# Halved loads and a re-ordered scatter in the expert loop of a two-block transformer kernel

## The reference

```
idx, gate = top 8 of 64 experts a token (4 of 8 groups), gates scaled to sum 2.5
y_rows    = (silu(xb @ w_gate[e]) * (xb @ w_up[e])) @ w_down[e] * gate      # 1024 -> 256 -> 1024
routed    = zeros(256, 1024).at[row_tok].add(y_rows)                        # the scatter
x         = x + g2 * (routed + shared(h))
out       = rmsnorm(x, final_g)
```

## Time and profile before

| | |
|---|---|
| median of 3 runs | 1319.68 us (1318.68 to 1320.43) |
| profiled execution | 1322.26 us, span 1320.6 us, mean granted clock 0.997 |
| TensorE busy | 1291.8 us (98%) |
| VectorE, ScalarE, GpSimd busy | 708.1, 254.1, 147.7 us |
| moved by DMA | 356.45 MB, mean 270 GB/s |

### The profile page before, as it was taken

How to read it: one execution, slowest core, us unless ns; L and a number is a source line. 1 busy time by engine, 2 the same in 40 slices (tenths; PEclk the granted TensorE clock), 3 DMA queues, 4 the chain that set the end, 5 groups by cost and what they waited for, 6 DMA issues and landing times.

```text
span 1320.6 us, 20050 instructions
## 1 busy us (share of the span) xinstructions
PE 1291.8 (98%) x7744; PEld 801.0 (61%) x7744; DVE 708.1 (54%) x1308; ACT 254.1 (19%) x586; POOL 147.7 (11%) x133
## 2 busy tenths in 40 slices
PE   9999999999999999999999999999999999999997
PEld 8667675875879566686685765744344444444432
DVE  1235589778789669968878574622222222222223
ACT  2144311201211251111122152310000000000002
POOL 1125500000011432000000902000000000000000
PEclk9999999999999999999999999999999999999999
DMA  9940154664533346675683414599999999999995
GB/s 381 362 155 34 65 194 168 244 226 176 204 126 130 142 177 243 248 301 194 262 310 147 154 70 169 222 420 420 420 421 421 421 420 420 421 421 421 420 422 224
DMA packets 51219, 356.45 MB, mean 270 GB/s; under 512 B 5936, under 2 KB 6208, under 8 KB 9536
## 3 DMA queue, kind: packets, MB, share of 16 engines
q1 hardware_dynamic: 45456, 321.45, 60.5%
q0 software_dynamic: 5392, 32.05, 6.6%
q10 hardware_dynamic: 288, 1.80, 0.3%
HBM read 353.73 MB, written 1.05 MB: 269 GB/s over the span
## 4 chain that ended last, share of the span: by engine, by line
PE 87%; DVE 7%; DMA 2%; issue 2%; ACT 1%; DVEq 0%; SPq 0%; ACTq 0%
PE ps L1089 13%; PE ps L1625 13%; PE ps L1080 11%; PE ps L1603 6%; PE ps L1654 6%; PE ps L1562 5%; PE ps L856 4%; PE ps L1370 4%; PE ps L1037 4%; PE ps L939 2%; PE ps L1019 2%; PE ps L1363 2%; PE ps L960 2%; DMA y_rows<-in_stream 2%; PE ps L895 1%
## 5 line engine op out<-in xcount | busy, mean ns | idle before, releaser
L3099 DVE TENSOR_TENSOR masked_and_probs<-ps,gate_rows 128x512 f32<-128x512 f32 x52 | 33.6, 686 | 143.9 <-PE ps L1654 142.5
L1603 PE MATMUL ps<-masked_and_probs,probT 128*128 128x512 f32 x208 | 94.4, 594 | 0.1
L3089 DVE TENSOR_TENSOR masked_and_probs<-masked_and_probs,ps 128x256 f32<-128x256 f32 x26 | 11.0, 421 | 153.9 <-ACT masked_and_probs L2163 153.9
L1080 PEld LDWEIGHTS ps<-xT,ring 128*128 128x128 f32 x768 | 87.7, 192 | 4.9 <-issue 4.9
L1080 PE MATMUL ps<-xT,ring 128*128 128x128 f32 x768 | 88.8, 275 | 0.8 <-issue 0.8
L1089 PE MATMUL ps<-ring,qk_tiles 128*128 128x512 f32 x192 | 85.2, 592 | 0.0
L1796 ACT ACTIVATE qk_tiles<-ps 128x512 f32<-128x512 f32 (+7 forms) x58 | 30.2, 522 | 256.4 <-PE ps L1080 248.5
L2163 ACT ACTIVATE masked_and_probs<-ps 128x256 f32<-128x256 f32 x26 | 10.0, 383 | 348.5 <-PE ps L1625 348.5
L1625 PE MATMUL ps<-ring,vec_rows 128*32 128x512 f32 (+2 forms) x312 | 64.9, 592 | 0.0
L1562 PE MATMUL ps<-masked_and_probs,mix_rows 128*128 128x256 bf16 (+1 forms) x384 | 61.9, 269 | 0.7 <-ACT v_rows L2139 0.7
L1089 PEld LDWEIGHTS ps<-ring,qk_tiles 128*128 128x128 f32 x192 | 35.8, 190 | 41.6 <-issue 41.6
(11 more groups left out here) (549 smaller groups left out, 2595.0 us busy)
## 6 DMA issues: line engine op xcount, KB each, us to landing
ring<-in_stream SPq DMA_DIRECT2D x201, 1024.0 KB, 9.9
qk_tiles<-in_stream SPq DMA_DIRECT2D x38, 1024.0 KB, 21.0
v_rows<-in_ada POOLq DMA_DIRECT2D x12, 1024.0 KB, 5.6
qk_tiles<-in_ada POOLq DMA_DIRECT2D x12, 1024.0 KB, 6.2
vec_rows<-in_stream SPq DMA_DIRECT2D x12, 1024.0 KB, 19.9
par<-in_stream SPq DMA_DIRECT2D x12, 1024.0 KB, 16.9
y_rows<-in_stream SPq DMA_DIRECT2D x12, 1024.0 KB, 17.3
xT<-in_stream SPq DMA_DIRECT2D x12, 1024.0 KB, 20.3
```

The source lines that it names most:

```text
L1080: mm = pe.matmul(ps[:, bank, m * P:(m + 1) * P], weights[:, kk, m * P:(m + 1) * P], tokens[:, kk, :], start=fresh and m == 0 and kk == 0, ...
L1603: mm = pe.matmul(ps[:, q, :], probT[:, buf, 256 + q // 2 * P:256 + (q // 2 + 1) * P], yslot[:, q % 2 * 512:(q % 2 + 1) * 512], start=False ...
L3099: dve.tensor_tensor(yslot[:, cols], ps[:, 5 + half, :], gaterow[:, 1, cols], ALU.mult).then_inc(ready, 1)
```

## The change

Four edits, all in or behind the loop:

- Loads. The up chunk comes in two row halves (all four first halves, then all four second halves; the second ones count in `s_rear`), with a wait in front of the products of its last two row groups. The halves of the down chunk are no longer row halves but column halves: each takes 512 columns of both k, so two runs of 2 KB a partition. 20 loads an iteration instead of 16, same bytes.
- Down by column halves. `down_units(half)` makes one half of the columns with both k; the second call waits for `s_second`.
- Scatter. Quarters 0 and 2 of the last static block go ahead of the loop, behind a wait for `s_ya`; 1 and 3 between gate and up. Quarters 0 and 2 of the loop's own rows go between the two down halves, behind waits for `s_tsb` and `s_ya`; 1 and 3 come behind the next iteration's gate products, or behind the loop. The gather, the transposes and the waits for the copies have no scatter beside them any more.
- Final squares and gains run in the order 0, 2, 1, 3; one semaphore replaces two.

```diff
+        s_rear = sem("rear_rows_loaded")
...
-                for n in range(2 * PER_MORE):
-                    c, a = divmod(n, PER_MORE)
-                    sp.wait_ge(s_late, it * LOOPED + (n + 1))
-                    load(LOOP_SLOTS[n][0], ids[a] * 3 + (RINGED + c))
+                for a in range(PER_MORE):
+                    sp.wait_ge(s_late, it * LOOPED + (a + 1))
+                    load(LOOP_SLOTS[a][0], ids[a] * 3 + RINGED)
                 for half in range(2):
                     cols = slice(half * D, (half + 1) * D)
+                    for a in range(PER_MORE):
+                        slot = LOOP_SLOTS[PER_MORE + a][0]
+                        if half == 0:
+                            sp.wait_ge(s_late, it * LOOPED + (PER_MORE + a + 1))
+                        sp.dma_start(moe_slot(slot)[:, cols],
+                                     d_stream[bass.ds(ids[a] * 3 + (RINGED + 1), 1)].rearrange("o p c -> (o p) c")[:, cols]
+                                     ).then_inc(s_rear if half else m_full[slot], 16)
+                for half in range(2):
+                    cols = slice(half * 512, (half + 1) * 512)
                     for a in range(PER_MORE):
                         n = 2 * PER_MORE + a
                         slot = LOOP_SLOTS[n][0]
                         if half == 0:
                             sp.wait_ge(s_late, it * LOOPED + (n + 1))
-                        sp.dma_start(moe_slot(slot)[:, cols],
-                                     d_stream[bass.ds(ids[a] * 3 + (RINGED + 2), 1)].rearrange("o p c -> (o p) c")[:, cols]
+                        sp.dma_start(moe_slot(slot).rearrange("p (k n) -> p k n", k=2)[:, :, cols],
+                                     d_stream[bass.ds(ids[a] * 3 + (RINGED + 2), 1)].rearrange(
+                                         "o p (k n) -> (o p) k n", k=2)[:, :, cols]
                                      ).then_inc(s_second if half else m_full[slot], 16)
...
-            def scatter(buf, quarters=range(4), last=False):
+            def scatter(buf, quarters=range(4)):
                 for q in quarters:
-                    if last and q == 1:
-                        pe.wait_ge(s_yv, more + NB)
                     mm = pe.matmul(ps[:, q, :], probT[:, buf, 256 + q // 2 * P:256 + (q // 2 + 1) * P],
                                    yslot[:, q % 2 * 512:(q % 2 + 1) * 512], start=False, stop=False, skip_group_check=True)
-                    if last:
-                        mm.then_inc(s_moe, 1)
+                return mm
...
-            def down_units(slots, buf, it):
-
+            def gate_up_units(slots, it):
+
+                pe.wait_ge(s_hga, it + (2 * PAIRS + 1))
+                pe.wait_ge(s_hgv, it + (2 * PAIRS + 1))
+                for c in range(2):
+                    ws = []
+                    for a in range(PER_MORE):
+                        slot, full = slots[c * PER_MORE + a]
+                        pe.wait_ge(m_full[slot], full)
+                        ws.append(moe_slot(slot).rearrange("p (k n) -> p k n", k=4))
+                    for kk in range(4):
+                        if c == 1 and kk == 2:
+                            pe.wait_ge(s_rear, it * (16 * PER_MORE) + 16 * PER_MORE)
+                        for a, ((lo, width),) in enumerate(UNIT_TILES):
+                            mm = pe.matmul(ps[lo:lo + width, 4, :], hg[:, 4 * c + kk, lo:lo + width], ws[a][:, kk, :],
+                                           start=c == 0 and kk == 0, stop=c == 1 and kk == 3, skip_group_check=True)
+                            if kk == 3:
+                                mm.then_inc(s_late, 1)
+                    if c == 0:
+                        pe.wait_ge(s_yv, it + NB)
+                        scatter(act_buf, (1, 3))
+
+            def down_units(half, slots, buf, it):
+
+                if half:
+                    pe.wait_ge(s_second, it * (16 * PER_MORE) + 16 * PER_MORE)
                 ws = []
-                for a, tiles in enumerate(UNIT_TILES):
+                for a in range(PER_MORE):
                     slot, full = slots[2 * PER_MORE + a]
                     pe.wait_ge(m_full[slot], full)
                     ws.append(moe_slot(slot).rearrange("p (k n) -> p k n", k=2))
                 for k in range(2):
-                    if k == 1:
-                        pe.wait_ge(s_second, it * (16 * PER_MORE) + 16 * PER_MORE)
-                    for half in range(2):
-                        for a, ((lo, width),) in enumerate(UNIT_TILES):
-                            mm = pe.matmul(ps[lo:lo + width, 5 + half, :], probT[:, buf, k * P + lo:k * P + lo + width],
-                                           ws[a][:, k, half * 512:(half + 1) * 512], start=k == 0, stop=k == 1,
-                                           skip_group_check=True)
-                            if k == 1:
-                                mm.then_inc((s_downhalf, s_late)[half], 1)
+                    for a, ((lo, width),) in enumerate(UNIT_TILES):
+                        mm = pe.matmul(ps[lo:lo + width, 5 + half, :], probT[:, buf, k * P + lo:k * P + lo + width],
+                                       ws[a][:, k, half * 512:(half + 1) * 512], start=k == 0, stop=k == 1,
+                                       skip_group_check=True)
+                        if k == 1:
+                            mm.then_inc((s_downhalf, s_late)[half], 1)
...
             act_buf = (NB - 1) % 2
+            pe.wait_ge(s_tsb, NB)
+            pe.wait_ge(s_ya, NB)
+            scatter(act_buf, (0, 2))
             with pe.Fori(0, more) as it:
                 slots = [(slot, it * 16 + 16 * (loads + 1)) for slot, loads in LOOP_SLOTS]
                 pe.wait_ge(s_tsb, it * 2 + NB)
                 pe.wait_ge(s_sel, it + (PAIRS + 1))
                 gather_units()
-                pe.wait_ge(s_ya, it + NB)
-                pe.wait_ge(s_yv, it + NB)
-                scatter(act_buf, range(1))
-                pe.wait_ge(s_hga, it + (2 * PAIRS + 1))
-                pe.wait_ge(s_hgv, it + (2 * PAIRS + 1))
-                gate_up(UNIT_TILES, slots, [s_late] * LOOPED, [hg[:, 0:4, :], hg[:, 4:8, :]])
-                scatter(act_buf, range(1, 3))
+                gate_up_units(slots, it)
                 pe.wait_ge(s_hid2, it + (NB + 1))
                 turn_hidden_rows().then_inc(s_tps, 1)
-                scatter(act_buf, range(3, 4))
-
                 turn_weights(unit_selectw, 4).then_inc(s_tps, 1)
                 pe.wait_ge(s_tsb, it * 2 + (NB + 1))
-                down_units(slots, act_buf, it)
-            pe.wait_ge(s_ya, more + NB)
-            pe.wait_ge(s_tsb, more * 2 + NB)
-            scatter(act_buf, last=True)
+                down_units(0, slots, act_buf, it)
+                pe.wait_ge(s_tsb, it * 2 + (NB + 2))
+                pe.wait_ge(s_ya, it + (NB + 1))
+                scatter(act_buf, (0, 2)).then_inc(s_moe, 1)
+                down_units(1, slots, act_buf, it)
+            pe.wait_ge(s_yv, more + NB)
+            for q in (1, 3):
+                scatter(act_buf, (q,)).then_inc(s_moe, 1)
...
-                act.wait_ge(s_moe, q + 1)
...
-            for q in range(4):
-                square_quarter(q)
+            act.wait_ge(s_moe, more)
+            square_quarter(0)
+            square_quarter(2)
+            act.wait_ge(s_moe, more + 1)
+            square_quarter(1)
+            act.wait_ge(s_moe, more + 2)
+            square_quarter(3)
             std()
-            act.wait_ge(s_root, 1)
-            act.wait_ge(s_gained, 3)
+            act.wait_ge(s_gained, 4)
             for t in range(TT):
                 first_half_out(t)
...
-            def gain_quarter(q):
+            def gain_quarter(q, squares):
                 t, cols = q // 2, slice((q % 2) * 512, (q % 2 + 1) * 512)
-                dve.wait_ge(s_ss, 5 + q + 1)
+                dve.wait_ge(s_ss, 5 + squares)
                 dve.tensor_tensor(y[:, t, cols], ps[:, q, :], vec[:, 1, cols], ALU.mult).then_inc(s_gained, 1)
             link(dve.memset(guard, RMS_EPS))
             dve.wait_ge(s_vecA, 64)
             dve.wait_ge(s_vecB, 80)
-            for q in range(3):
-                gain_quarter(q)
+            gain_quarter(0, 1)
+            gain_quarter(2, 2)
+            gain_quarter(1, 3)
             link(dve.tensor_tensor(guarded, quarter_ms[:, :, 0], guard.to_broadcast([P, TT]), ALU.add))
             dve.wait_ge(s_ss, 5 + 4)
             norms[0] += 1
             dve.tensor_tensor(var2, quarter_ms[:, :, 1], guarded, ALU.add).then_inc(s_var, 1)
             dve.wait_ge(s_std, norms[0])
             inv_sqrt(rstd, var2, std2, nwt)
-            dve.engine_nop().then_inc(s_root, 1)
+            dve.engine_nop().then_inc(s_gained, 1)
             dve.wait_ge(s_gained, 3)
```

More of the change, by code:

```diff
@@ L424, in build @@
         s_gated = sem("shared_down_gated")
-        s_root = sem("last_inverse_roots")
-        s_gained = sem("last_rows_by_gain")
```

(1 more changed line is left out.)

## The result

The changed kernel took 1326.64 us in the median of 5 runs (1324.84 to 1329.47), the kernel before, beside it, 1320.13 (1318.68 to 1320.43): ratio 1.0054, 95% interval 1.0039 to 1.0069, so 6.5 us between the medians. Run twice more it gave 1.0052 (1.0039 to 1.0066) and 1.0053 (1.0040 to 1.0067). The forecast was 1325.5, range 1323.2 to 1328.2.

What follows compares the result with a forecast made beforehand. The prediction took the order of TensorE's own work, not the loads, to bound the kernel. Its terms 2.71 + 0 + 1.72 - 0.64 + 1.99 gave +5.8 us on the median 1319.68: 1325.5 us, range 1323.2 to 1328.2.

Steps and rivals of the forecast that it cites:

- Bound: End of the kernel: the order of TensorE's own work sets the end; weight loads are early by 3.4 and 1.8 us.
- Step 1: Ahead of the loop: a 0.99 us wait for VectorE's half plus four scatter slots delay the gather, +2.71 us.
- step 3: Gate to up: four scatter slots now stand between the products, their waits long met, +1.72 us.
- step 4: End of up to start of down: no scatter fills it, the dependent chain takes 2.58 instead of 3.22 us, -0.64.
- step 5: Down halves and scatter alternate: TensorE needs each half right after making it, 4.59 us a leg, +1.99 us.
- second sum, by waits: TensorE's idle time grows by 0.99, 0.86 behind the gather, about 2.1 around transposes, 2 x 1.15 less 0.29 at the end.
- Step 7: Loads: 2 KB segments at some 385 GB/s, last landing 1306.5, needed at 1314.1, 0 us; upper bound 1.8.
- Rival D: Loads: 2 KB segments run at half rate or worse, +1.8 us on top, 1327.3 us; chance 0.03.
- step 2: Gather to gate: stays 4.89 us though emptied of scatter, 0 us; bounds -0.49 and +0.2.
- rival A: New tail: short gaps halve TensorE's clock, losing 1.5 us (1327.0) to 6.9 us (1332.4); chance 0.10.
- Rival B: Loop's second-half loads: the last landing sets the end, so the change gains 0.86 us, 1318.8 us; chance 0.04.
- Rival C: Three waits for VectorE's halves (0.99, 1.15, 1.15) cost nothing, leaving +2.5 us, 1322.2 us; chance 0.06.

Runs made afterwards that it cites:

- experiment 2: Kernel before with the change's loads and merged semaphore, TensorE's old order kept: 1320.50 us against 1320.50, ratio 1.0001.
- 3: Changed kernel with the loads of the kernel before, so only the new order of work: 1325.54 us against 1320.50, ratio 1.0036.
- 4: Changed kernel with quarters 0 and 2 of the last static block moved between gather and gate: 1323.56 us against 1320.33, ratio 1.0024.
- 6: Changed kernel with quarters 1 and 3 behind the up products instead of between gate and up: 1324.06 us against 1320.33, ratio 1.0029.
- 5: Changed kernel with the two down halves back to back, quarters 0 and 2 behind them: 1324.41 us against 1320.33, ratio 1.0031.
- 10: Changed kernel with all scatter quarters set into existing waits and down halves back to back: 1319.74 us against 1320.50 before, ratio 0.9997.
- experiment 9: Changed kernel plus six small ScalarE copies lengthening the gap between gather and gate: 1325.49 us against 1320.22 before, ratio 1.0047.
- experiment 7: Changed kernel plus two unread 128x512 products between gather and gate, run twice: 1326.31 and 1326.27 us, ratios 1.0042 and 1.0048 to before.
- experiment 11: Changed kernel with scatter quarters in existing waits, down halves together, final squares released one by one: 1318.36 us against 1320.22 before, ratio 0.9989.

## Why the prediction was right

Measured step by step in the trace of the changed kernel against the one before:

| step | forecast | measured | from |
|---|---|---|---|
| 1 quarters 0, 2 ahead of the loop | +2.71 | +2.79 | gather from 0.16 us ahead of VectorE's half to 2.63 behind it |
| 2 gather to gate | 0 | -0.10 | 4.89 to 4.79 |
| 3 quarters 1, 3 between gate and up | +1.72 | +1.95 | 7.00 to 8.95 (1296.76 to 1305.71) |
| 4 end of up to down | -0.64 | -0.97 | 3.22 to 2.25 (1305.71 to 1307.96) |
| 5 down, scatter, to the last square | +1.99 | +2.14 | 7.48 to 9.62 (1307.96 to 1317.58) |
| sum | +5.8 | +5.81 | |

- *Bound.* Right: with TensorE's old order the new loads changed nothing (experiment 2), and with the old loads the new order carried the effect (3).
- *Step 1* is confirmed by its undoing (4: -2.78), *step 3* with the wait of step 4 behind it (6: -1.40), *step 5* by 5: -2.30 from the start of down. Together these are -6.48; the filled order (10), which puts all these pieces back into waits, has -6.72 against the change and is no slower than before. The times agree: 3.2, 4.1 and 3.7 us above before in experiments 4, 5 and 6, where 5.8 less what each one took off at the end of its chain leaves 3.0, 3.8 and 4.4, all inside the intervals.
- *Step 3* was 0.23 short. The scatter among the side-by-side products started 0.14 us late (1300.34 for a slot due at 1300.20), and the products behind it 0.19 (1302.25 for 1302.06); 0.1 of such a switch stands in the 7.00 of before as well. *Step 4* was too cautious by 0.33: I let the copy's wait of 0.56 stand in full, it is 0.12 of "issue" behind the copy. That a sum of five terms came out within 0.03 is luck: they were off by +0.08, -0.10, +0.23, -0.33 and +0.15. The prediction's second sum, by waits, in fact adds up to 5.96.
- *Step 7* was right in rate (377 GB/s in the window of 2 KB segments, 385 estimated) and in time: the last landing, moved by the 1.4 us, is 1306.3, estimated 1306.5. *Rival D* is out with it.
- *What was mis-sized is step 2's upper bound (+0.2)*, and how I set up rival A. I had put the fall of the clock in the last stretch, as a world of its own with a chance of 0.10. It happens in part of the executions, in the gap that step 2 emptied: of the seven traces in which nothing stands between gather and gate (three of the change, experiments 3, 5, 6, 9) four show it, of the seven in which something does (before and experiments 2, 4, 7 twice, 10, 11) none. If the filling made no difference, all four would fall among the seven empty ones by chance in 35 of 1001 arrangements, 3.5%. It costs 1.4 to 1.7 us when it comes. The 15 runs of the change average 1327.2 and the 10 with the filled gap 1326.1, against 1320.3 before: 6.9 and 5.8 us, and the second is the forecast sum. Half of 1.7 us, 0.85, is near the 1.1 us between the two. That it is the whole surplus is argued and not shown, since the intervals of the times overlap and experiment 9 did not sort itself as expected.
- *What the fall needs* is open in part. All seven empty traces also have the stop of 0.93 us ahead of the scatter, some 5 us sooner. That stop alone does not do it, since experiment 7 has it twice without a fall; whether the gap alone would is open, as no kernel has the empty gap without the stop.
- The Trainium skill ("TensorE: Matmul & The Clock Gate", section "A second HAM failure mode: psum-queue depth-cycling") was nearer than I gave it credit for: it says that short idles of TensorE between groups of products, when they come often enough, make the clock go up and down. The traces agree in part: behind the gap of 1.95 us, with the stop of 0.93 ahead of it, the clock fell in some executions; behind the later stops of 0.9 to 1.2 us none of the traces shows a fall before the last matmul.
- *Rival B* was out at the forecast's dates. In experiment 11 the landing does hold TensorE up, for 0.3 us: there the second down half is due 7.5 us sooner than in the change, counted from VectorE's first half.
- *Rival C* of the prediction, that the three waits for VectorE are covered, is out: the stops of 0.93, 0.98 and 0.89 us stand bare in the chain.

## What to carry to other kernels

Where one engine carries the chain, moving its independent pieces changes nothing in the sum of its work and everything in its stops: list each wait of that engine with its length, and set independent pieces of that length there. A piece placed ahead of a wait rather than in it is paid in full, and the wait that it leaves empty stays as long as it was (here 1.72 us for quarters 0 and 2 and 0.93 for a new stop for their input, with 4.79 us from gather to gate where there were 4.89); halves that are used right after they are made need other work between making and using. Splitting transfers can help only where a landing is the last thing waited for, so look for that first.

## What the hardware showed that I had not expected

- Behind an empty gap of 1.95 us, with a stop of 0.93 us some 5 us ahead of it and products all around, TensorE went to 1.2 GHz for about 3 us in some executions and not in others of the same program.
- Small ScalarE copies in a row cost 0.08 us each (six of 30 columns lengthened the gap by 0.5 us, 1.95 to 2.47), though one is recorded as some 0.2 us.
- The time from issue to landing of a 512 KB load fell from 17.4 us with 4 KB rows to 11.0 with 2 KB runs, at 408 and 377 GB/s in the windows shown. Fewer bytes can have been ahead of it in the full queue; no run tested that.
